# A two-block transformer kernel: the ring places after the second expert stage, and the last pair of experts loaded in halves

## The reference

```
first block:   h = rms_norm(x);  z = h @ w_in -> attention, gated spatial unit, gates
               x += merged @ w_out;  x += cross_attention(x, mem)
               x += moe(rms_norm(x))                      # 16 experts, 2 per token   (stage 1)
second block:  for i in 0, 1:
                 shift, scale, gate = silu(c) @ ada_w[i, 0] + ada_b[i, 0]
                 h = x * (1 + scale) + shift
                 y = stick_breaking(h) if i == 0 else retention(h)
                 x = layer_norm(ALPHA * x + (1 + gate) * y)
                 shift, scale, gate = silu(c) @ ada_w[i, 1] + ada_b[i, 1]
                 h = x * (1 + scale) + shift
                 y = moe(h)                               # 16 experts, 2 per token   (stages 2 and 3)
                 x = layer_norm(ALPHA * x + (1 + gate) * y)

moe: for each expert e:  y += combine[:, e] * ((silu(t @ w_gate[e]) * (t @ w_up[e])) @ w_down[e])
```

## Time and profile before

| | |
|---|---|
| median of 3 runs | 1453.13 us |
| the profiled execution | 1459.76 us |
| its span, first to last instruction | 1457.9 us |
| mean granted TensorE clock | 0.971 of full speed |
| PE busy | 1310.4 us, 90% of the span |
| DVE, ACT, POOL busy | 572.4, 432.8, 407.8 us |
| read from memory | 445.38 MB, 306 GB/s over the span |
| chain of waits: share of PE, of DMA, of DVE | 63%, 19%, 9% |
| stage 1, 2, 3: last pair's first wait for weights ends | 476.78, 904.52 us; none in stage 3 |

### The profile page before, as it was taken

One profiled execution on the slowest core, in us unless ns is written; L12 is line 12 of the kernel. 1 busy time (PEld: TensorE's weight loads), 2 busy tenths in 40 slices (PEclk: granted clock), 3 DMA queues, 4 the chain that ended last, 5 costly groups with the idle time before them and its releaser, 6 DMA issues.

```text
span 1457.9 us, 20767 instructions
## 1 busy us (share of the span) xinstructions
PE 1310.4 (90%) x7694; PEld 811.8 (56%) x7695; DVE 572.4 (39%) x1234; ACT 432.8 (30%) x693; POOL 407.8 (28%) x190
## 2 busy tenths in 40 slices
PE   6999998889899899998889898599998979998985
PEld 5887787533334398775333343289886853343422
DVE  5598555522112143446223222367007062421224
ACT  4554443211111145543111111145444332111110
POOL 5893643000000077051000000169964710000000
PEclk9999999999999999999999999899999999999988
DMA  9664568899999984429499999796635479999961
GB/s 356 204 210 176 189 232 319 357 389 416 428 427 428 406 323 174 174 101 408 167 379 426 428 427 428 294 340 228 220 126 205 164 325 394 419 425 428 428 271 58
DMA packets 89628, 448.04 MB, mean 307 GB/s; under 512 B 7804, under 2 KB 9768, under 8 KB 70952
## 3 DMA queue, kind: packets, MB, share of 16 engines
q1 hardware_dynamic: 85856, 445.87, 76.8%
q10 hardware_dynamic: 3656, 0.57, 0.3%
HBM read 445.38 MB, written 1.05 MB: 306 GB/s over the span
## 4 chain that ended last, share of the span: by engine, by line
PE 63%; DMA 19%; DVE 9%; ACT 3%; issue 3%; POOL 2%; SPq 0%; DVEq 0%; ACTq 0%; POOLq 0%
PE ps L430 61%; DMA ring_hi<-in_moe_w_up 10%; DMA ring_lo<-in_w_up 7%; POOL WLO L2563 1%; DMA ring_lo<-in_ada_w 1%; PE ps L452 1%; DVE Z L1979 1%; DVE Z L1967 1%; DVE Z L1980 1%; DVE Z L1978 1%; DMA ring_lo<-in_w_ckv 1%; PE ps L895 1%; POOL RS L2532 1%; ACT WHI L1362 0%; DVE ST L1808 0%
## 5 line engine op out<-in xcount | busy, mean ns | idle before, releaser
L2563 POOL TENSOR_TENSOR WLO<-ring_lo,WHI 128x1024 fp32r<-128x1024 f32 (+1 forms) x154 | 377.0, 2465 | 686.2 <-ACT WHI L1362 684.4
L430 PE MATMUL ps<-ring_lo,Z 128*64 128x512 f32 x1328 | 439.9, 610 | 30.4 <-DMA ring_hi<-in_moe_w_up 9.9
L430 PE MATMUL ps<-ring_hi,Z 128*64 128x512 f32 x1072 | 381.2, 606 | 22.3 <-DMA ring_lo<-in_w_up 8.9
L430 PEld LDWEIGHTS ps<-ring_lo,Z 128*64 128x64 f32 x1328 | 138.8, 140 | 229.8 <-issue 210.4
L1362 ACT ACTIVATE WHI<-ring_lo 128x1024 fp32r<-128x1024 f32 (+1 forms) x160 | 166.3, 1049 | 206.5 <-PE ps L430 191.2
L430 PEld LDWEIGHTS ps<-ring_hi,Z 128*64 128x64 f32 x1072 | 116.7, 139 | 161.1 <-issue 143.0
L2230 DVE TENSOR_TENSOR Z<-ps,Z 64x512 f32<-64x512 f32 x48 | 33.1, 689 | 342.2 <-ACT Z L1569 335.7
L1569 ACT ACTIVATE Z<-ps 64x512 f32<-64x512 f32 x48 | 28.4, 591 | 354.0 <-PE ps L430 354.0
L430 PE MATMUL ps<-WHI,HTH 128*128 128x512 f32 x320 | 126.4, 395 | 5.0 <-DVE HTL L2432 1.6
L430 PE MATMUL ps<-WLO,HTH 128*128 128x512 f32 x320 | 125.2, 391 | 0.0
L430 PE MATMUL ps<-WHI,HTL 128*128 128x512 f32 x320 | 125.1, 391 | 0.0
(11 more groups left out here) (297 smaller groups left out, 1708.3 us busy)
## 6 DMA issues: line engine op xcount, KB each, us to landing
ring_lo<-in_moe_w_gate SPq DMA_DIRECT2D x25, 2048.0 KB, 16.0
ring_lo<-in_ada_w SPq DMA_DIRECT2D x24, 2048.0 KB, 8.9
ring_hi<-in_moe_w_up SPq DMA_DIRECT2D x23, 2048.0 KB, 18.5
ring_lo<-in_moe_w_down SPq DMA_DIRECT2D x17, 2048.0 KB, 17.4
ring_lo<-in_w_up SPq DMA_DIRECT2D x16, 2048.0 KB, 19.9
ring_hi<-in_moe_w_down SPq DMA_DIRECT2D x15, 2048.0 KB, 13.8
ring_lo<-in_ret_w_in SPq DMA_DIRECT2D x12, 2048.0 KB, 9.0
ring_hi<-in_w_gate SPq DMA_DIRECT2D x10, 2048.0 KB, 16.5
```

Of the source, the lines that this page charges most:

```text
L430: return nc.tensor.matmul(o, l, r, start=start, stop=stop, skip_group_check=True)
L2563: nc.gpsimd.tensor_tensor(WLO[:, q, 0:size], slot(r)[:, q * size:(q + 1) * size], WHI[:, q, 0:size].bitcast(F32), ALU.subtract).then_inc(S ...
```

## The change

Three parts. The counter of the dense panels moves on by two places behind the second stage only (`LEFT_FIRST`), so that the first panels there get the places of gate and up blocks, which PE has read earlier, rather than those of down blocks. In each stage the last pair's six loads become twelve of 1 MB: gate and up are cut along the features (chunks 0 to 3, 4 to 7), down along the output columns. The first halves have semaphores of their own (`half_even`, `half_odd`, `half_down`), and PE waits for the second halves in the middle of its work. For this SP's loop is shortened by one turn, and its two pairs are written out. The third part only merges semaphores of the start of the program, to make room for the three new ones: `silu_c` and `mask_ready` become `act_constants`, `angles` and `qk_roped` become `rope_ready`.

```
+    LEFT_FIRST = (0, 2, 0)
     LOADS = ((0, 0), (0, 1), (1, 0), (1, 1), (0, 2), (1, 2))
...
             expert_slot.append(expert_slots(key[1], turn_d))
+            turn_d += LEFT_FIRST[key[1]]
...
-                pe.wait_ge(S("silu_c"), 1)
+                pe.wait_ge(S("act_constants"), 2)
...
+                def second_half(a):
+
+                    def wait(c):
+                        if c == KC // 2:
+                            for j in range(2):
+                                pe.wait_ge(landed[s[a][j]], at(a, j))
+                    return wait
...
-                    for j in range(2):
+                    if final:
+                        pe.wait_ge(S(("half_even", "half_odd")[a]), 32 * (L + 1))
+                    for j in range(0 if final else 2):
                         pe.wait_ge(landed[s[a][j]], at(a, j))
...
-                            chunks_in if first and a == 0 else None)
+                            chunks_in if first and a == 0 else second_half(a) if final else None)
...
-                for a in range(2):
+                if final:
+                    pe.wait_ge(S("half_down"), 32 * (L + 1))
+                for a in range(0 if final else 2):
                     pe.wait_ge(landed[s[a][2]], at(a, 2))
                 down_half(banks[1], 0, wd)
+                for a in range(2 if final else 0):
+                    pe.wait_ge(landed[s[a][2]], at(a, 2))
...
+        def load_half(L, e, r, j, h, done):
+
+            w = MOE_W[L][j][e:e + 1].rearrange("o (p c) n -> p (o c) n", p=P)
+            to = slot(r).rearrange("p (c n) -> p c n", n=w.shape[2])
+            part = (slice(None), slice(None), slice(512 * h, 512 * h + 512)) if j == 2 else (slice(None), slice(4 * h, 4 * h + 4))
+            sp.dma_start(to[part], w[part]).then_inc(done, 16)
+
+        def load_last(L, waits, slots):
+
+            for parts, first in ((((0, 0), (0, 1)), "half_even"), (((1, 0), (1, 1)), "half_odd"), (((0, 2), (1, 2)), "half_down")):
+                for h in range(2):
+                    for a, j in parts:
+                        if h == 0:
+                            waits(a, j)
+                        load_half(L, NE - 2 + a, slots[a, j], j, h, landed[slots[a, j]] if h else S(first))
...
-            with sp.Fori(1, NE // 4) as i:
...
+            with sp.Fori(1, NE // 4 - 1) as i:
+                load_pair(4 * i, 0)
+                load_pair(4 * i + 2, 1)
+            load_pair(NE - 4, 0)
+            load_last(L, lambda a, j: slot_left(NE - 2, 1, a, j), expert_slot[L][3])
```

More of the change, by code:

```diff
@@ L706, in attention @@
             values(heads - 1)
-        pe.wait_ge(S("qk_roped"), 1)
+        pe.wait_ge(S("rope_ready"), 2)
         transposes("gq", lambda t, c: QR[:, t, c * P:(c + 1) * P], 4)
@@ L1118, in sb_values @@
                     fill(mm(o[k][half_rows(h), 128:256], SBV[:, 1, 64 * h:64 * h + 64], SE[:, h, 256:384], False, True), ("sv", h))
-            pe.wait_ge(S("mask_ready"), 1)
+            pe.wait_ge(S("act_constants"), 1)
             logits("z2", 0, False)
@@ L1277, in _, with slot_left, load_pair @@
                     load_expert(L, e + a, place[key, n][0], j)
-            with sp.Fori(1, NE // 4) as i:
[L1279 to L1296, removed]
+            def slot_left(e, k, a, j):
+                if (a, j) == (0, 0):
+                    blocks(L, e - 2, 0)
+                if (a, j) == (1, 0):
+                    blocks(L, e - 3, 2)
+                if (a, j) == (1, 1):
+                    blocks(L, e - 1, 1)
+                if (a, j) == (1, 0) and k == 0:
+                    wait_moe(sp, L, "y", e - 2)
+                    sp.wait_ge(m(L, "xdone"), blocks_done[2])
+                elif (a, j) == (1, 0):
+                    wait_moe(sp, L, "gu", e - 2)
+                    sp.wait_ge(m(L, "x_gu"), blocks_done[2])
+                else:
+                    wait_expert_read(L, e + (a - 2), a, j)
+            def load_pair(e, k):
+                for a, j in LOADS:
+                    slot_left(e, k, a, j)
+                    load_expert(L, e + a, expert_slot[L][2 + k][a, j], j)
+            with sp.Fori(1, NE // 4 - 1) as i:
[3 more added lines that the diff above has]
+            load_last(L, lambda a, j: slot_left(NE - 2, 1, a, j), expert_slot[L][3])
             if L:
@@ L1406, in _ @@
         nc.scalar.activation(MASK[:, 0, :], ident, Copy)
-        nc.scalar.activation(MASK[:, 1, :], cst(C_NEGMASK), Copy).then_inc(S("mask_ready"), 1)
-        nc.scalar.activation(SILC[:, :, :], bc(VT[:, 0, V_C:V_C + 8], [8, 32], 2), ACT.Silu).then_inc(S("silu_c"), 1)
+        nc.scalar.activation(MASK[:, 1, :], cst(C_NEGMASK), Copy).then_inc(S("act_constants"), 1)
+        nc.scalar.activation(SILC[:, :, :], bc(VT[:, 0, V_C:V_C + 8], [8, 32], 2), ACT.Silu).then_inc(S("act_constants"), 1)
         split_next(("ckv", 1))
@@ L1417, in _ @@
         split_next(("in", "kv"))
-        act.wait_ge(S("angles"), 1)
+        act.wait_ge(S("rope_ready"), 1)
         nc.scalar.activation(CS2[:, 0, :], RR[:, 0, :], ACT.Sin)
@@ L1913, in _ @@
         link(V.tensor_scalar(RR[:, 0, :], RR[:, 0, :], np.pi / 2, None, ALU.add))
-        V.tensor_scalar(RR, RR, 3.1415925, -3.1415925, ALU.min, ALU.max).then_inc(S("angles"), 1)
+        V.tensor_scalar(RR, RR, 3.1415925, -3.1415925, ALU.min, ALU.max).then_inc(S("rope_ready"), 1)
         def ada_add(n):
@@ L1984, in _ @@
                 ins = V.tensor_copy(kd[:, :, r, :], R5[:, t, 512:640].rearrange("p (v d) -> p v d", v=2))
-        ins.then_inc(S("qk_roped"), 1)
+        ins.then_inc(S("rope_ready"), 1)
         for t in range(NT):
```

## The result

The changed kernel runs in 1447.93 us (median of 10, 1445.98 to 1450.47), the kernel before beside it in 1456.73 (median of 10, 1452.17 to 1460.33): a ratio of 0.9942, 95% interval 0.9928 to 0.9956, or -8.8 us. Forecast were 1443 us in a range of 1436 to 1452, and a sum of -10.3.

A forecast was written before the change was run, and what follows sets the result against it. PE was taken to bound the kernel, with transfers setting the pace in the middle of the stages. From the median 1453.1 us, -2.8 behind stage 1 and -7.5 behind stage 2 (-10.3) gave 1442.8, so 1443; range 1436 to 1452.

The forecast's parts named there:

- sum of -10.3: Whole kernel: -2.8 us behind stage 1, -7.5 behind stage 2, 0 in stage 3 and for the merged semaphores.
- the forecast's own range: Whole kernel: 1439 to 1447 us for the main forecast without its rivals, given a chance of 0.58.
- the base: Whole kernel: the time before the change from which the sum was taken off, a median of 1453.1 us.
- the side of the largest chance: Whole kernel: faster, below 1445.8 us, chance 0.69; slower had 0.04, no change to be told 0.27.
- Seam 2: Behind stage 2: panel 18 lands at 938.9 rather than 946.34, projection starts at 950.0 rather than 957.49, -7.5 us.
- The stream with halves: Last pairs' loads: down halves at 387 GB/s, +1.0 us per stage; gate and up halves +0.2; no cost per transfer.
- neither slower rival: Added transfers at 2.8 us each, 1476 us, chance 0.08; or the skill page's 7.4 us a stage, 1458, no change.
- The rival of a small cost per transfer: Last pairs' loads: 0.4 us per small transfer, 2.4 us on each seam, 1447.6 us in all; chance 0.18.
- Seam 1: Behind stage 1: PE's tail ends earlier but meets the stream; projection at 516.1 rather than 518.87, -2.8 us.
- panel 11's landing would bind: Behind stage 1: panel 11 lands at 513.7, after the turned rows (514 at the latest), and sets the projection's start.
- the halves' 3.55 us: Last pairs on PE: half of one expert's 7.10 us of gate and up, by which PE's tail ends earlier.
- Seam 3: Last pair of stage 3: PE waits for no block, so halves give nothing and their cost is hidden, 0 us.

The follow-up runs named there:

- experiment 1: The kernel before with only the dense panels' turn moved on by two behind stage 2, all loads whole: 1447.86 us, ratio 0.9942.
- Experiment 6: The changed kernel with five unused products on constants ahead of panels 10 and 18, filling PE's idle time: 1449.42 us, ratio 0.9943.
- 2: The changed kernel with the dense panels' turn as before, last pairs still in halves: 1451.97 us, ratio 0.9976 to the kernel before.
- Experiment 3: The changed kernel with the last pair's down blocks loaded whole, gate and up still as halves: 1446.69 us, ratio 0.9933.
- 5: Kernel 4 with POOL making the norms' roots ahead of the first quarter of the projection panel's low split: 1448.83 us, ratio 0.9943.
- kernel 8: Kernel 5 with ACT's copy of the modulation panel's result ahead of its high split of the projection panel: 1450.64 us, ratio 0.9951.
- kernel 10: Kernel 3 (down blocks whole) with the filling products of kernel 6 ahead of panels 10 and 18: 1447.83 us, ratio 0.9936.
- kernel 4: The changed kernel with modulation panels 10 and 18 loaded ahead of the first projection panel of their section: 1453.91 us, ratio 0.9990.
- 7: The changed kernel with the edits of kernels 3, 4 and 5 together: 1451.65 us, ratio 0.9972 to the kernel before.
- Kernel 9: Kernel 8 with both modulation panels of a seam (10 and 11, 18 and 19) loaded ahead of the projection panel: 1455.55 us, ratio 0.9986.

## Why the prediction was nearly right

The time lies in the range, 4.9 us above the number and 0.9 above the forecast's own range of 1439 to 1447. Of that, 3.6 us is the base: the three runs shown had a median of 1453.1, the ten beside the changed kernel (those three among them) 1456.7. The sum itself is off by 1.5: -10.3 against -8.8. The prediction called a time below 1445.8 faster, counted from the same low base; against its own base the kernel is 0.58% faster (interval 0.44 to 0.72), a little more than the 0.5% it asked for, and so on the side of the largest chance.

**Seam 2: right, mechanism and size.** -7.5 was predicted, and -7.1 is the difference of the distances. Each step is in the rows: the panel's load 15.3 us earlier, counted from the last up block; a wait of 6.16 us (6.3 counted); the landing 24.8 us behind the last up block (24.3 counted); the clock fallen in that wait, and panel 18 at 5.78 us as at 5.75 before; 11.2 us from there to the projection (11.15).

**The stream with halves: right.** 418 to 423 GB/s for gate and up halves between the two bounds, and close to the upper one, as taken: 8.4 MB at 421 and at 426 GB/s differ by 0.23 us, against the 0.2 of the sum. 385 to 387 for down halves. The share of the DMA engines never fell below 1 between them. The Trainium skill ("DMA: Bandwidth & Descriptors", section "Bandwidth") has 341 GB/s for a transfer of 1 MB; this trace shows 418 to 423 for 1 MB transfers that follow one another in a full queue, so its figure does not carry over, and neither slower rival came true. The rival of a small cost per transfer gave 1447.6, the measured time almost to the digit, and is wrong all the same: six times 0.4 us would show as landings 2.4 us late, and panels 10 and 18 land 1.1 and 0.5 us later than counted. That leaves room for 0.2 us a transfer at most; no run separates such a cost from other reasons for the 1.1.

**Seam 1: the term that was mis-sized.** -2.8 was predicted, -1.4 is there, and experiment 1, which has no halves, also stands about 1.2 below the kernel before: the halves as such brought some 0.2 us, by one profile each. The base was one execution in which the clock had fallen on expert 15's products (8.78 us for 7.10); that 1.7 us was counted as a gain of the halves, and other executions lack it without any. And two sizes behind it were too small. Panel 10 lands 22.8 us behind the last up block (488.82 + 18.96 against 463.46 + 21.55), where 21.7 were counted: 1.1 us late. The rate is not the reason: over that time the windows show 375 to 394 GB/s, which is 8.8 MB, more than the 8.4 of the four blocks. What it is stays open. And I let the clock fall only where it did no harm: I said that panel 10 might take 3.9 us and that panel 11's landing would bind at any rate. It took 3.64, the rows followed, and the chain from there (the turned rows, then 1.91 and 0.60 us of DVE) ends at 516.03, later than panel 11 (513.73 + 1.96) would have allowed. Experiment 6 confirms the second size: with the clock up panel 11's landing does bind (its own wait is 1.57 us), and the distance is 0.8 us shorter.

**What I did not see: the two parts share one gain.** The sum gave each seam one cause. At seam 2 it took the halves' 3.55 us as real PE time and let them end in the wait for panel 18, and that is what happened (6.16 us of wait, where 3.55 less would be left without the halves). The step that would have told more was left out: what each part gives when the other is away. Experiments 1 and 2 show it, and so the halves are worth nothing that the medians can tell beside the places (1447.93 and 1447.86), though 4.6 us without them. Experiment 3 says the same for the down blocks alone.

**Seam 3: right.** PE waits for no block in the last pair of stage 3, and the cost of halves there is hidden.

**What stays open.** The two distances together give the medians' gains to within 2 us for the changed kernel and for kernels 1, 2, 3, 5, 8 and 10. Kernels 4 and 7 are 3.3 and 3.5 us slower in the median than their profile's distances say. Kernel 9 is 5.8 slower, and 3.3 of that stand just behind the first products (experiment 9). Kernel 6 is 5.3 slower, its profile being of its fastest run. Between executions of one kernel the places at which the clock falls move, in the whole program and not only at the seams, and one profile for each kernel can't settle that.

## What to carry to other kernels

When a load waits for a buffer, look first at who used that buffer last: giving the panel a place that PE had read some 20 us earlier cost one number and brought the whole gain. Before adding up the gains of two edits at one seam, ask which of them still finds a wait to shorten when the other is in; an experiment with each alone is cheap. And of several blocks wanted at once, send first the one that passes through other engines on its way (the projection panel, split by ACT and POOL; no other order tried here was faster), and look at what is queued behind that work on those engines before turning the order around: kernel 4 was 6 us slower than the changed kernel, and 5 of them came back when POOL's roots no longer stood behind the split.

## What the runs showed of the hardware beyond that

**An issue can take long.** SP's rows for the last pair's down halves are 0.6, 0.6, 7.8 and 2.8 us long in the chain of the changed kernel, where most whole blocks take 0.33 to 0.43; the first gain row behind them took 2.49. The same blocks in one transfer each are issued in 0.80 us for both (experiment 3). It is not a matter of halves alone: panel 18, one transfer of 2 MB with 2 KB rows, took 6.37 us to issue in the changed kernel and 15.09 in kernel 3, and in the kernel before a projection panel issued at 937.48 took 5.43. In these cases several MB were already in the queue. The down halves have 2 KB rows like the panels, so there are more pieces for the same bytes (the page counts 96829 packets against 89628 before, and 91357 with the down blocks whole); that SP waits for room for them is a guess, which no run tested. It cost nothing here, since the stream stayed full. Where SP had something urgent behind such a load it might cost, which no run here shows.

**Two clock levels, wandering.** Over windows of 2.5 us I summed what the granted clock lacks to full speed: 42 us before, 36 in the changed kernel, 34 to 39 in kernels 1, 5, 7 and 10, and 19 in kernel 6's run of 1441.6 us (busy or not, so not all of it is PE's loss). Taking away one idle time did not always take away the fall: in kernel 6's profile it is gone at both seams, in kernel 10's it stands some 10 us earlier, in the down products, and in kernel 8's it lies on panel 19 rather than on the rows ahead of it.
